# Decoder trunk step: the first three units of the input projection taken from the unnormalised input and scaled per token afterwards

## The reference, cut to what matters

```
xn = x * rsqrt(mean(x * x, axis=-1) + EPS) * norm1_g
z  = xn @ w_in + b_in
u, q, k, v, o, ipre, fpre, ga, gb = split(z)
uc = causal_dwconv(u)                    # width 4
ha = rg_lru(uc)                          # gates from uc @ block-diagonal weights, then a scan
```

## Time and profile before

| | us |
|---|---|
| median of 3 runs | 1062.01 |
| lowest and highest | 1061.0, 1062.16 |
| the profiled execution | 1065.16 |
| its span | 1063.4 |

### The profile page before, as it was taken

One profiled execution on the slowest core, in us unless ns is written; L12 is line 12 of the kernel. 1 busy time (PEld: TensorE's weight loads), 2 busy tenths in 40 slices (PEclk: granted clock), 3 DMA queues, 4 the chain that ended last, 5 costly groups with the idle time before them and its releaser, 6 DMA issues.

```text
span 1063.4 us, 19336 instructions
## 1 busy us (share of the span) xinstructions
PE 1051.9 (99%) x7912; PEld 1024.8 (96%) x7912; DVE 640.6 (60%) x976; ACT 385.8 (36%) x557; POOL 372.4 (35%) x183
## 2 busy tenths in 40 slices
PE   8999999999999999999999999999999999999997
PEld 6899999999999999999999999999999999999997
DVE  5778357964534464362643339999940189999313
ACT  6566787313332334232422343222211122222332
POOL 4323333333222222232123434444433343334330
PEclk8999999999999999999999999999999999999999
DMA  7443332376378595783452233222323222333312
GB/s 198 152 111 84 96 93 80 90 194 166 86 214 220 126 261 126 191 240 90 149 172 81 80 100 99 80 80 80 102 82 95 60 80 80 87 91 98 94 43 90
DMA packets 246464, 126.08 MB, mean 119 GB/s; under 512 B 67915, under 2 KB 242235, under 8 KB 246126
## 3 DMA queue, kind: packets, MB, share of 16 engines
q1 hardware_dynamic: 246172, 124.82, 42.9%
q10 hardware_dynamic: 210, 0.07, 0.0%
HBM read 100.62 MB, written 22.04 MB: 115 GB/s over the span
## 4 chain that ended last, share of the span: by engine, by line
PE 98%; ACT 1%; DMA 1%; DVE 0%; issue 0%; SPq 0%; DVEq 0%
PE ring L2107 48%; PE ring L2502 22%; PE bank L2502 17%; PE bank L2373 2%; PE bank L2360 1%; PE bank L2341 1%; PE bank L2353 1%; PE bank L2414 1%; PE bank L2268 1%; PE bank L2402 1%; PE bank L2154 1%; DMA x_tok<-in_x_prompt 1%; PE ring L2145 0%; PE bank L2548 0%; ACT sq_tok L1036 0%; PE bank L2166 0%
## 5 line engine op out<-in xcount | busy, mean ns | idle before, releaser
L2107 PE MATMUL ring<-x_split,whi 128*128 128x256 f32 (+1 forms) x2016 | 358.9, 300 | 0.0
L934 POOL TENSOR_TENSOR wlo<-stage,whi 128x1024 fp32r<-128x1024 f32 x78 | 194.9, 2499 | 405.8 <-ACT whi L999 405.8
L2107 PEld LDWEIGHTS ring<-x_split,whi 128*128 128x128 f32 x2016 | 304.2, 189 | 9.1 <-issue 8.6
L2107 PE MATMUL ring<-x_split,wlo 128*128 128x256 f32 (+1 forms) x1008 | 217.5, 297 | 0.0
L2107 PEld LDWEIGHTS ring<-x_split,wlo 128*128 128x128 f32 x1008 | 169.9, 189 | 0.0
L999 ACT ACTIVATE whi<-stage 128x1024 fp32r<-128x1024 f32 x80 | 84.2, 1053 | 93.9 <-PE ring L2107 79.3
L984 POOL TENSOR_TENSOR wlo<-stage,whi 128x1024 fp32r<-128x1024 f32 x28 | 71.9, 2567 | 107.6 <-ACT whi L1334 107.6
L2502 PE MATMUL ring<-x_split,whi 128*128 128x256 f32 (+1 forms) x512 | 88.7, 295 | 0.0
L1450 DVE SCALAR_TENSOR_TENSOR conv<-up,cols,conv 128x592 f32<-128x592 f32 x88 | 77.5, 881 | 3.1
L2502 PEld LDWEIGHTS ring<-x_split,whi 128*128 128x128 f32 x512 | 77.0, 189 | 0.0
L2013 DVE TENSOR_SCALAR conv<-up,cols 128x592 f32<-128x592 f32 x44 | 70.0, 1590 | 3.1
(11 more groups left out here) (367 smaller groups left out, 2059.6 us busy)
## 6 DMA issues: line engine op xcount, KB each, us to landing
stage<-in_w_in SPq DMA_DIRECT2D x56, 512.0 KB, 4.3
stage<-in_w_up SPq DMA_DIRECT2D x44, 512.0 KB, 3.8
stage<-in_w_down SPq DMA_DIRECT2D x16, 704.0 KB, 4.5
stage<-in_w_branch_a SPq DMA_DIRECT2D x8, 512.0 KB, 3.8
c_sample<-in_state_mlstm_C SPq DMA_DIRECT2D x16, 256.0 KB, 7.3
out_s_mlstm_C<-c_sample SPq DMA_DIRECT2D x16, 256.0 KB, 2.4
stage<-in_w_branch_b SPq DMA_DIRECT2D x8, 512.0 KB, 4.0
stage<-in_w_out SPq DMA_DIRECT2D x8, 512.0 KB, 3.8
```

Source lines behind the costliest of these rows:

```text
L934: pool.tensor_tensor(spaced(wlo[:, slot]), packed(stage[:, slot, 0:n]), spaced(whi[:, slot]).bitcast(F32), ALU.subtract).then_inc(w_lo, 1)
L2107: last = pe.matmul(of(z, t0 or -2, t1), w[:, kk * WS:kk * WS + P], x_, start=kk == 0 and m == 0, stop=kk == kn - 1 and m == 2)
```

## The change

Units 0, 1 and 2 (RAW = 3) are multiplied with the raw input: the gain goes into the high and low part (`raw_high`: xh = round(x_raw x gain); `raw_low`: xl = x_raw x gain - xh), r doesn't. Their results are multiplied by `rrow` when they leave the banks (`u_scaled`, VectorE), and ScalarE adds the bias behind it (`add_bias`). Unit 2 takes its weight from a third slot (whi3, wlo3). During unit 2, step by step as it has used them (`x_used`), xh is replaced by the rounded normalised input: `xn` = x_raw x gain x r is made by VectorE for feature tiles 0 to 4, x_raw x r by GpSimd for 5 to 7; `xn_high` rounds, and the low parts are made by GpSimd for tiles 0 and 1 and by VectorE for 2 to 7. Unit 3 starts on these, step by step (`xn_split`). The rms rows are spread during unit 2, the row transposes stand in it, the gate products behind it. Weight 1 is loaded ahead of the third token tile, weight 3 goes into the free slot 1 as soon as weight 1's low part is made, the LRU turns move from 3 and 6 to 5 and 7, the gate sums ahead of unit 4. The raw copies of jobs 4 to 7 and 12 to 15 go from ScalarE to VectorE. The diff's core:

```diff
-LRU_TURN = (3, 6, 9, 11, 13, 15, 17, 19)
+LRU_TURN = (5, 7, 9, 11, 13, 15, 17, 19)
...
-            for i in range(TT):
+            for i in range(2):
+                load_tile(x_tok, x_in, i)
+            load(1, 1, w_in, slice(0, P))
+            for i in range(2, TT):
                 load_tile(x_tok, x_in, i)
...
+            sp.wait_ge(w_lo, 1)
+            load(3, 1, w_in, slice(2 * P, 3 * P))
...
+                if p <= 1:
+                    sp.wait_ge(xn_lo, 2)
...
+            lo(1, 1, D)
...
+            pool.wait_ge(tile_evicted, T_XN + XN)
+            pool.wait_ge(rb_ready, 2)
+            for f in range(5, 8):
+                pool.tensor_tensor(xn[:, f], x_raw[:, f], rrow[:, :], ALU.mult).then_inc(xr_scaled, 1)
+            lo(4, 0, D)
+            for f in range(2):
+                pool.wait_ge(xn_hi, f + 1)
+                pool.tensor_tensor(xl[:, f], xn[:, f], xh[:, f].bitcast(F32), ALU.subtract).then_inc(xn_lo, 1)
+            los(5, B_WA + 3, D)
...
+            def raw_low(n):
+
+                f, t0, t1 = job(n)
+                dve.wait_ge(xr_hi, n + 1)
+                mul_add(xl[:, f, t0:t1], x_raw[:, f, t0:t1], cols[:, C_N1 + f:C_N1 + f + 1], xh[:, f, t0:t1].bitcast(F32),
+                        ALU.mult, ALU.subtract).then_inc(xr_lo, 1)
...
+            dve.wait_ge(rb_ready, 2)
+            u_scaled(0)
+            u_scaled(1)
+            for f in range(5):
+                mul_add(xn[:, f], x_raw[:, f], cols[:, C_N1 + f:C_N1 + f + 1], rrow[:, :], ALU.mult, ALU.mult
+                        ).then_inc(xn_scaled, 1)
+            u_scaled(2)
...
+            for kk in range(KT):
+                last = split_product(wide[(T_U + 2) % 2], None, KT, xh, xl, ks=[kk], weight=(whi3[:, :], wlo3[:, :]), m0=0)
+                last.then_inc(x_used if kk < KT - 1 else tile_done, 1)
+                if kk == 0:
+                    rms_rows(0)
+                    rms_rows(1)
+                elif kk == 4:
...
+                    row_transposes(wide[(T_U + 3) % 2], *COL_GROUPS[0])
+                elif kk == 6:
+                    pe.wait_ge(tile_evicted, T_RAW + 1)
+                    row_transposes(bank2(0), *COL_GROUPS[1])
             gate_products()
```

More of the change, by code:

```diff
@@ L86 @@
 XN = 16
-T_COLS2 = T_XN + XN
-T_U = T_COLS2 + 2
+RAW = 3
+T_RAW = T_XN + XN
+T_COLS2 = T_RAW + 2
+T_U = T_COLS2
 T_GA = T_U + 8
@@ L481, in of_first, with z_raw, spread_bank @@
             return z[:, SPLIT + t0:SPLIT + t1]
+        def z_raw(g):
+            return bank2(g)[:, SPLIT - BEGIN:] if g < 2 else wide[(T_U + g) % 2]
+        def spread_bank(part):
+            return ring[:, (T_U + 3) % 2, part]
         def ring_bank(n):
@@ L955, in _ @@
                                ALU.mult).then_inc(w_lo, 1)
-            for n in range(2, 8):
-                xn_low(n)
             sel_ = gate_sel[:, :]
@@ L1241, in gate_evict @@
                                ).then_inc(gate_evicted, 1)
-            for g in range(31):
-                if g:
-                    lru_period(g)
-                if g == 2:
+            for f in range(4):
+                xn_high(f)
+            hi(5, 1, D, T_RAW + 1, loads_of(5))
+            for f in range(4, 8):
+                xn_high(f)
+            act.wait_ge(lam_abs, 1)
+            act.activation(lam[0], lam[0], ACT.Exp, scale=-1.0).then_inc(lam_exp, 1)
+            for g in range(RAW):
+                add_bias(g)
+            for g in range(RAW, 31):
+                lru_period(g)
+                if g == 4:
                     gate_evict()
@@ L2147, in turn, with raw_step @@
                 return last
-            def part_step(z, M, step, wh, wl, kk, part):
-                f, t0, t1 = job(8 * part + kk)
-                pe.wait_ge(xn_lo_b if part else xn_lo, kk + 1)
-                for m, (w, x) in enumerate(((wh, xh), (wh, xl), (wl, xh))):
-                    last = pe.matmul(of_first(z, t0, t1)[0:M], w[:, step * kk:step * kk + M], x[:, f, t0:t1],
+            def raw_step(g, part, kk):
+                n = 8 * part + kk
+                f, t0, t1 = job(n)
+                slot = (B_U + g) % 2
+                pe.wait_ge(w_lo, 3 if g else 1)
+                pe.wait_ge(xr_lo, n + 1)
+                for m, (w, x) in enumerate(((whi, xh), (whi, xl), (wlo, xh))):
+                    last = pe.matmul(of_first(bank2(g), t0, t1), w[:, slot, WS * kk:WS * kk + P], x[:, f, t0:t1],
                                      start=kk == 0 and m == 0, stop=kk == KT - 1 and m == 2)
@@ L2197, in rms_rows @@
                     m = P if i < TT - 1 else LAST
-                    if i == 1:
-                        keep_clock(5)
                     pe.wait_ge(diag_done, i + 1)
-                    last = pe.matmul(bank[:, 3 - part, P * (i - tiles[0]):P * (i - tiles[0]) + m], ones[0:m, :],
+                    last = pe.matmul(spread_bank(part)[:, P * (i - tiles[0]):P * (i - tiles[0]) + m], ones[0:m, :],
                                      diag[i][0:m, 0:m], start=i == tiles[0], stop=True, skip_group_check=True)
                 last.then_inc(rb_psum, 1)
-            rms_rows(0)
             keep_clock(6)
```

299 lines of the change are left out of this document (154 added, 145 removed).

## The result

| | us |
|---|---|
| before, median of 4 runs | 1061.78 (1061.00 to 1062.16) |
| changed, median of 4 runs | 1075.20 (1074.15 to 1075.95) |
| changed, the profiled execution | 1075.09, span 1073.3 |
| ratio changed to before | 1.0129, 95% interval 1.0116 to 1.0142 |
| forecast | 1069.7, range 1059.5 to 1075.5 |

The changed kernel is 13.4 us slower. The forecast had the direction and a little over half the size.

A forecast was written before the change was run, and what follows sets the result against it. TensorE was taken as a matmul stream without a hole behind its start. The 5.6 us gained there is lost to port locking: unit 3 ends +6.0, convolution 0 waits 1.7, so 1062.01 + 7.7 = 1069.7 us, range 1059.5 to 1075.5.

The forecast's parts named there:

- First step near 14: Start of unit 0: TensorE's first step at about 14.0 us, 5.6 us ahead of 19.62.
- Raw stretch: 11 to 36.5 us: low parts delayed by GpSimd's subtractions on the shared port, clock 0.50 from about 15, unit 2 at 36.5.
- Replacement stretch by adding both engines' durations: 36.5 to 61 us: VectorE and GpSimd as one queue, sum 20.65 us; unit 3 ends at 60.9, +6.0.
- Wait of 1.7 us for convolution 0: Ahead of block 0's gates: convolution 0 ends at 70.3, TensorE arrives at 68.6 and waits 1.7 us.
- Unit 5 at 72.4, +7.7: Unit 5 starts at 72.4 us against 64.66 in the trace before, so the change costs 7.7 us.
- After that VectorE is busy about 60% and catches up.: Behind unit 5: VectorE, busy about 60%, catches up, so nothing is added to the +7.7 us.
- rival 1: Milder lock, VectorE keeping the port over its low parts: unit 2 at 34.0, unit 5 at 67.5, +2.8, 1064.8 us; chance 0.18.
- 2: No change: GpSimd's subtractions fall into VectorE's gaps; unit 2 at 33.0, unit 5 at 64.7, 1062.0 us; chance 0.13.
- 3: Faster: the operations don't exclude each other or the port costs nothing; unit 5 at 60.0, -4.7, 1057.3 us; chance 0.19.
- The upper end (4): Waits inside unit 3 take the clock to 0.50: up to +10.5, 1072.5 us; two blocks 1075; within the forecast's 0.50.

The follow-up runs named there:

- second profile of before: The kernel before, unchanged, profiled a second time: 1061.18 us.
- experiments 2 and 3: Changed kernel with GpSimd's three scalings and two low parts replaced by memsets: 1072.67 us; with those three scalings given to VectorE, all work kept: 1074.09 us.
- scan_first: Changed kernel with block 0's scan ahead of convolution 7 in VectorE's queue instead of behind it: 1071.24 us.
- experiment 8: Changed kernel with 24 extra transposes in the wait for low part 8 and 23 extra matmuls in unit 3's waits: 1075.21 us.
- experiment 6: The kernel before with block 0's scan moved ahead of convolution 7 on VectorE: 1061.38 us, ratio to before 1.0001.

## Why the prediction came out as it did

- **First step near 14.** 13.47. The weight landed at 8.8 instead of 10.0. Right, though against the second profile of before it is a gain of 5.0 us (18.46) and not of 5.6.
- **Raw stretch: unit 2 at 36.5, lows lengthened to 2 to 3 us in places.** 34.57. Both blocks are there: one low part of 2.49 at 19.93, beside weight 2's subtraction, and one of 2.69 at 24.67, beside the third slot's. But the last low part was ready at 28.3 instead of 30.3, and the clock was 1.00 from 15 to 20 us and 0.75 from 20 to 25, where the forecast had 0.50 from about 15. The forecast was 1.9 us too late.
- **Replacement stretch by adding both engines' durations.** From unit 2's start until TensorE reaches the gates of block 0 the forecast had 32.1 us, measured were 32.2. The parts were less exact, and partly it is luck. From both rows to the last new low part the forecast had 21.3 us (38.8 to 60.1), measured were 19.4 (37.1 to 56.5): the sum was 1.8 us too large. But unit 3 ended 2.4 us behind that low part and not 0.83: its last wait came earlier (4.1 us of waits in all, not 6.7), and the steps behind it ran at half clock. The mechanism, one port for the operations of two engines, is shown by experiments 2 and 3. Here it is read from rows: five operations 9.98 us beside GpSimd, 5.96 with its reads gone, 5.13 with its scalings on VectorE. The Trainium skill's rule (SBUF — State Buffer, SBUF: two separate sides) of an exclusive lock for the whole instruction agrees with these.
- **Wait of 1.7 us for convolution 0.** Absent. Convolution 0 ended at 66.4, with one block of 2.4 in the rates as forecast: 9.9 us behind the last new low part, where the forecast had 10.2. TensorE came 10.3 us behind it, and not 8.5, since unit 3 ended late. It was close: in eight of the variants TensorE waits 0.56 to 0.57 us there.
- **Unit 5 at 72.4, +7.7.** It came at 68.62, 3.8 us too early, and the mark of before that it was subtracted from was 3.7 us too late (64.66 in the profile with the half clock, 60.92 in the other). The difference, +7.7, is exact by two errors that cancel, which is luck. Its two terms weren't right either: against the second profile unit 3 ends 7.7 us late and not 6.0, and convolution 0 adds nothing and not 1.7. The step that failed here was to take a profiled execution 3.15 us above the median as the ground of marks and to carry only the difference to the median; the half clock in the earlier trace rows was the sign that this execution was not typical.
- **"After that VectorE is busy about 60% and catches up."** This is the step that failed. The 60% was an average over the whole span. Between 65 and 215 us VectorE is the engine whose queue holds the chain, and the share there rose, in the second profile of before and in the changed kernel (length, PE, PEld, DVE busy, and so on):

```profile
65.00:215.00 150.00, 150.00 (x1160) 144.00 (x1159) 108.63 (x140) 97.20 (x124) 56.01 (x21) 1.00 0.37 93
```

```profile
65.00:215.00 150.00, 146.33 (x1119) 139.24 (x1118) 126.93 (x143) 103.25 (x132) 51.82 (x21) 1.00 0.34 89
```

  From 72% to 85%: by 65 us four convolutions had begun before, and one after the change. TensorE waits 3.67 us in this stretch (1.44, 0.25 and 1.99) and 0.87 for merged at 226.95, 4.5 in all; the forecast had put what lies behind unit 5 at nothing. In the profiled execution of scan_first these waits are gone and with them 5.4 of the 5.7 us, so most of the 1.2 us that the four waits don't cover goes with them too. At the longest wait, 1.99 us, a matmul starts 2.30 us behind the one ahead of it where 0.13 is usual, so TensorE loses more there than the wait says. For the last 0.3 us I have no row.
- **Rivals.** 1 and 2 had the port milder than it was, 3 had no lock at all; experiments 2 and 3 rule out 3. The marks of the changed kernel lie nearer to rival 1 (unit 2 at 34.0, convolution 0 at 65.4, unit 5 at 67.5) than to the forecast, but not for its reason: VectorE didn't keep the port over its series of low parts (the 2.69 us at 24.67), and weight 5's subtraction came at 49.17, ahead of VectorE's new low parts. The upper end (4), half clock inside unit 3, did occur, at a clock of 0.82 and 0.83, and cost 0.3 us at most by experiment 8. The time landed inside the range, at its upper end, for another reason than the one given for it: that is luck too.

## What to carry to other kernels

When work moves later on an engine, read its busy share in the stretch where it will land, not over the span, and follow who waits for the operations queued behind: one scan behind one convolution was worth nothing in one kernel and 4 us in the other. Two engines that lock each other out are one queue, so giving work to the second made the first slower than doing it all alone. And before marks are taken from a profile, compare its own time with the median: here one that was 3 us above the median had its marks 3.7 us late.

## What the runs showed of the hardware

- Five 128x592 operations of VectorE with two inputs took 9.98 us beside five of GpSimd's that read SBUF, and eight took 7.2 beside two. Even an operation of 128x8 elements took 2.41 us when it met GpSimd's subtraction (0.17 otherwise): here it is the length of the other's instruction that counted. The row, and the GpSimd row that it met:

```profile
60.25 2.41 DVE L1620 TENSOR_TENSOR misc<-misc 128x8 f32<-128x8 f32 x1
...
60.23 2.40 POOL L952 TENSOR_TENSOR wlo<-stage,whi 128x1024 fp32r<-128x1024 f32 x1 [8.70 <-ACT whi L1018]
```

- The same program had, in one execution, half clock for some 7 us near its start and in another none there: 1065.16 and 1061.18 us. The kernel of experiment 6 had such a profiled execution too (1064.30 us, granted clock 0.51 between 20 and 25 us) beside a median of 1061.38.
- Half clock in unit 3, where TensorE waits for other engines, cost 0.3 us at most (gates of block 0 at 66.78, convolution 0 done at 66.44); with it and without it the kernel took 1075.20 and 1075.21 us.
